# Unread 512-column matmuls in TensorE's two waits between the last output projection and the expert tables

## The chip, the cores and the metric

The kernel runs on one core of one Trainium2 chip. The metric is device time in microseconds (us) of one launch. The kernel before took 2901.69 us (median of 3 runs, 2897.95 to 2902.46).

## The reference

One layer of a streaming encoder over 4096 prompt frames and 8 streams of 16 sample frames, all in float32 with 1024 channels. What it computes, cut to what matters:

```python
h = rms_norm(x, norm1_g)
z, xbc, dt, gu, gv = split(h @ w_in)
xbc, conv_new = causal_conv(xbc, conv_prev)          # silu, width 4
y, h_final = ssd_scan(xs, dt, a, B, C, h0)           # 8 heads x 64, state 128
ssd_out  = group_rmsnorm(y * silu(z)) * ssm_norm_g
gmlp_out = gelu(gu) * (tril(W_s) @ layer_norm(gelu(gv)) + b)
x = x + concat(ssd_out, gmlp_out) @ w_out            # output projection
h2 = rms_norm(x, norm2_g)
# hierarchical MoE: top-1 of 4 groups, then top-2 of 8 SwiGLU experts in it
expert, weight = route(h2)
x = x + sum_k weight_k * (silu(h2 @ w_gate[e_k]) * (h2 @ w_up[e_k])) @ w_down[e_k]
y = rms_norm(x, final_norm_g)
```

Besides y it returns the convolution tails, the final states of the scan (`ssm_prompt`, `ssm_sample`) and the sample streams' v rows.

## The kernel before, in words

The program is written out by hand for each engine, with semaphores between the engines; nothing reorders it. It has two stages.

Stage 1 goes over 33 tiles of 128 tokens (32 of the prompt, one of the 8 sample streams). In each turn TensorE projects the next tile (`project`, `project_channels`), runs the scan and the spatial gate of this one, and ends with the output projection (`pe_out`, three blocks of columns, of which the last, YB, also holds the router's logits). VectorE adds the residual (`dve_x2`, L888), ScalarE sums the squares (`act_x2sq`, L731), GpSimd takes the root (L1134), and VectorE then picks the experts of the tile (`dve_route`, L1003 to L1026). TensorE counts the picks by two small matmuls, the rank (`pe_rank`, L532 and L533), and VectorE turns the counts into places in the experts' token lists (`dve_slots`, L1034 to L1048), which GpSimd scatters to memory.

The end of stage 1, where the change lies, is `pe_end` on TensorE. After the last output projection it runs two of the eight matmuls of the sample streams' new states (`pe_sample_update`, L553), the rank of the last tile, and the third of those matmuls. Meanwhile VectorE goes through `dve_route` and `dve_slots` for the last tile and then `dve_tables`: from the final counts it works out which 128-token block belongs to which expert. GpSimd gathers the token lists (L1480) once `row_i` is there. TensorE turns the table columns `tcol` into rows (`pe_table_rows`, L1590), waits for the lists, transposes these too (L1597), and runs the other five state matmuls, each of which waits for VectorE to have read an older one (`smp_new`, L1080). VectorE copies the tables (L1434), does three steps of the state update (L1079 and L1080), writes the lists (L1438 to L1440), and the rest. When tables and lists are there, GpSimd gathers the first blocks' rows (L1488).

Stage 2 goes over pairs of blocks of 128 slots, for at least 33 pairs, and further pairs by a branch: TensorE transposes the gathered rows (`pe_rows`, L1566), multiplies by gate and up (`pe_gate_up`, L1581, 8 matmuls of 512 columns) and by down (L1621). The expert weights arrive in four slots of SBUF by SyncE's queue; the first three experts' are loaded while stage 1 ends.

The PSUM bank that the change writes, `TB_mem[:, 0]`, is read for the last time in stage 1 by ScalarE before the last output projection, and is written next by L1566. `ident` and `cst` are constants in SBUF, loaded at the start. Each matmul of float32 in the program stands as two records, each with its own weight load, in the trace; a transpose stands as one.

Of the kernel before, what the change touches and what calls it, by code (L numbers as in the profile page):

```python
# [109 lines left out]
def after(eng, sem, n):  # L110

    if n > 0:
        eng.wait_ge(sem, n)
# [8 lines left out]
def build(nc, x_rows, x_cols, consts_in, cols_in, bcast_in, w_in, w_out, w_out_T_in, ws_in, ws_smp_in, cache_in, st_old_in,  # L122
          st_T_in, slot_in, w_exp, final_g, y_out, conv_prompt, ssm_prompt, conv_sample, ssm_sample, gmlp_v_sample):
    ctx = ExitStack()
    with ctx:
        def sb(name, shape, dt=F32):
            return ctx.enter_context(nc.sbuf_tensor(name, shape, dt))

        def ps(name, shape):
            return ctx.enter_context(nc.psum_tensor(name, shape, F32))  # L130
# [4 lines left out]
        def flat(ap):  # L135
            return ap.rearrange("p a b -> p (a b)")
# [25 lines left out]
        cst = sb("cst", [P, NCONST])  # L162
        ident, tri, stri, tri_s = (cst[:, c:c + P] for c in (C_IDENT, C_TRI, C_STRI, C_TRI_S))
# [79 lines left out]
        TB_mem = ps("TB", [P, 2, 4, P])  # L243
# [87 lines left out]
        def half(b):  # L331
            return slice(4 * b, 4 * b + 4)
# [133 lines left out]
        def pe_turn(pe, tn):  # L466
            i, u = tn.i, tn.u
            v = 1 - u
            if tn.end:
                pe_end(pe)  # L470
                return
# [54 lines left out]
        def pe_rank(pe, i, after_decay, cb_read):  # L526

            pe.wait_ge(s["pick_ready"], i)
            pe.wait_ge(s["cb_read"], cb_read)
            if after_decay:  # L530
                pe.wait_ge(s["smp_dec_out"], 1)
            nc.tensor.matmul(rk_p, stri, oh[:, 2, :], start=True, stop=True)  # L532
            nc.tensor.matmul(cnt_p, ones[:, 0:1].broadcast_to([P, P]), oh[:, 2, :], start=True, stop=True).then_inc(s["rank_done"], 1)  # L533
# [15 lines left out]
        def pe_sample_update(pe, n0, n1):  # L549

            for n in range(n0, n1):
                after(pe, s["smp_new"], n - 2)
                nc.tensor.matmul(smp_bank[n % 3], xw[:, (n // 2) * P:(n // 2 + 1) * P],  # L553
                                 flat(bmask[:, n // 4, half(n % 2), :]), start=True, stop=True).then_inc(s["states_done"], 1)

        def pe_end(pe):
            pe.wait_ge(s["smp_masks"], 3)
            pe.wait_ge(s["gated_ready"], NT)
            pe_sample_update(pe, 0, 2)
            pe_rank(pe, NT, False, NT)  # L560
            pe.wait_ge(s["lg_read"], NT)
            pe_sample_update(pe, 2, 3)

        def pe_phase1(pe):
            pe.wait_ge(ident_loaded, 16)
            pe_spread(pe, 0, TB[0], [])
            project_channels(pe, 0, 0, "xa", "proj_xa", [("x_scaled", 1)], by_block="xa_scaled")
            pe_spread(pe, 1, TB[0], [])
            project_channels(pe, 0, 1, "xb", "proj_xb", [("w_scaled", 1)])
            project(pe, 0, PB[0][:, 0:NVA], "va", "proj_va", [("w_scaled", 2), ("xa_out", 1)])  # L570
            project(pe, 0, PB[1][:, 0:NVB], "vb", "proj_vb", [("w_scaled", 3), ("xb_evicted", 1)])
            pe_router_weights(pe, 0)
            project(pe, 0, PB[0][:, :], "u", "proj_u", [("w_scaled", 4), ("va_out", 1)])
            pe_router_weights(pe, 1)
            project(pe, 0, PB[1][:, :], "z", "proj_z", [("w_scaled", 5), ("gv_out", 1)])
            pe.wait_ge(const_loaded, 16)
            pe_front_sums(pe, 0)
            pe_router_weights(pe, 2)
            pe_front_channels(pe, 0)
            over_tiles(lambda tn: pe_turn(pe, tn))  # L580
# [1271 lines left out]
```

## Time and profile before

| | |
|---|---|
| median of 3 runs | 2901.69 us |
| the profiled execution | 2901.85 us |
| its span | 2900.0 us |
| around the span | 1.85 us |
| mean granted clock | 0.992 of full |
| PE busy | 2855.1 us (98%) |
| VectorE busy | 1580.9 us (55%) |
| GpSimd busy | 870.4 us (30%) |
| ScalarE busy | 807.8 us (28%) |

The share of an engine says how much of the span it was at work. The chain of waits follows the work that ended last back to the start; what stands in it lay on the path that sets the time. In the rows of single instructions the first number is the start in us from the span's start, the second the time that the group took. PEclk is the granted clock of TensorE as a share of 2.4 GHz: 0.50 is 1.2 GHz.

### The profile page before, as it was taken

To read this page: it belongs to the slowest core of one execution; us is meant where nothing else is said; L and a number is where in the kernel's file an instruction comes from. 1 tells how busy PE (TensorE), PEld (TensorE's weight loads), DVE (VectorE), ACT (ScalarE), POOL (GpSimd) and SP (SyncE) were. 2 spreads that over 40 slices of the span, in tenths; PEclk is the share of its full clock that TensorE was granted. 3 is DMA by queue.
4 is the path that set the end of the run, shared out by engine and by line. 5 is a ranking of instruction groups with operands and counts; after the bars stand their busy time and mean duration, and the time that the engine had idled before them with its cause. 6 is when DMAs were issued, how large, how long until landed. Compare 5 with 4: busy or idle time off the path is not lost.

```text
span 2900.0 us, 38336 instructions
## 1 busy us (share of the span) xinstructions
PE 2855.1 (98%) x12809; PEld 1888.1 (65%) x12809; DVE 1580.9 (55%) x4163; ACT 807.8 (28%) x1518; POOL 870.4 (30%) x1366
## 2 busy tenths in 40 slices
PE   8999999999999999999999999989999999999997
PEld 6776777677767767777777677754444444444443
DVE  5656565556555565556565656564444444444444
ACT  2223232322332232323232322312222222222222
POOL 0121111112111211121112112114656665656665
PEclk9999999999999999999999999989999999999999
DMA  7312121221112111211121211257675667567653
GB/s 308 140 52 73 59 73 52 73 73 60 54 71 80 52 59 66 80 52 62 70 74 52 73 60 65 75 221 267 236 262 191 224 200 255 200 219 269 245 171 124
DMA packets 109623, 369.01 MB, mean 127 GB/s; under 512 B 39497, under 2 KB 41426, under 8 KB 99442
## 3 DMA queue, kind: packets, MB, share of 16 engines
q1 hardware_dynamic: 48946, 252.91, 23.9%
q0 software_dynamic: 60480, 113.57, 11.9%
q8 instruction: 112, 1.84, 0.3%
q14 instruction: 85, 0.70, 0.1%
HBM read 325.09 MB, written 140.33 MB: 160 GB/s over the span
## 4 chain that ended last, share of the span: by engine, by line
PE 97%; DMA 1%; DVE 1%; issue 0%; SPq 0%; POOL 0%; ACT 0%; POOLq 0%; DVEq 0%; ACTq 0%
PE PB L368 24%; PE PB L1581 19%; PE PB L379 16%; PE PB L463 12%; PE SS L1621 9%; PE YB L463 4%; PE TB L1566 2%; PE YB L417 2%; PE TB L357 1%; DMA arena<-in_w_in 1%; PE SS L426 1%; PE TB L440 1%; PE SS L430 1%; PE TB L404 1%; PE YB L1614 1%; PE MB L408 1%
## 5 line engine op out<-in xcount | busy, mean ns | idle before, releaser
L368 PE MATMUL PB<-arena,hT 128*128 128x512 f32 (+2 forms) x2112 | 726.7, 498 | 1.5 <-ACT xT L592 0.8
L368 PEld LDWEIGHTS PB<-arena,hT 128*128 128x128 f32 x2112 | 398.3, 191 | 269.8 <-issue 224.3
L1581 PE MATMUL PB<-arena,hT 128*128 x1296 | 569.3, 592 | 0.0
L379 PE MATMUL PB<-hT,arena 128*128 128x128 f32 x4224 | 487.1, 276 | 4.2 <-DVE arena L1096 4.2
L379 PEld LDWEIGHTS PB<-hT,arena 128*128 128x128 f32 x4224 | 481.6, 193 | 8.1 <-issue 4.5
L1581 PEld LDWEIGHTS PB<-arena,hT 128*128 128x128 f32 x1296 | 246.4, 190 | 309.2 <-issue 309.2
L1133 POOL TENSOR_SCALAR rs<-sq 128x2 f32<-128x2 f32 (+1 forms) x66 | 14.1, 213 | 1306.6 <-ACT h L731 957.1
L463 PE MATMUL PB<-arena,tT 128*128 128x274 f32 (+1 forms) x1056 | 357.8, 493 | 0.7 <-ACT tT L636 0.7
L1621 PE MATMUL SS<-arena,xdt 128*128 x640 | 287.9, 593 | 0.0
L463 PEld LDWEIGHTS PB<-arena,tT 128*128 128x128 f32 x1056 | 195.7, 190 | 140.6 <-issue 120.4
L795 DVE SCALAR_TENSOR_TENSOR xc<-xT,cols,xc 128x128 f32<-128x128 f32 x792 | 216.8, 346 | 3.5
L1621 PEld LDWEIGHTS SS<-arena,xdt 128*128 128x128 f32 x640 | 115.5, 191 | 114.7 <-issue 114.7
L1651 ACT ACTIVATE xdt<-YB 128x256 f32<-128x256 f32 x80 | 30.8, 385 | 512.1 <-PE YB L1614 512.1
L1680 DVE TENSOR_TENSOR gv<-ycat,PB 128x256 f32<-128x256 f32 x81 | 34.1, 421 | 214.0 <-ACT ycat L1646 210.3
L731 ACT ACTIVATE h<-x_res 128x1024 f32<-128x1024 f32 x33 | 34.9, 1057 | 384.6 <-DVE x_res L888 384.6
L592 ACT ACTIVATE xT<-PB 128x512 f32<-128x512 f32 x64 | 38.2, 599 | 350.0 <-PE PB L379 350.0
L463 PE MATMUL YB<-arena,tT 128*128 128x274 f32 x528 | 127.6, 394 | 0.0
L793 DVE TENSOR_SCALAR xc<-xT,cols 128x128 f32<-128x128 f32 x264 | 70.8, 342 | 94.2 <-ACT xT L592 88.2
L463 PEld LDWEIGHTS YB<-arena,tT 128*128 128x128 f32 x528 | 100.0, 190 | 22.0
L1688 DVE SCALAR_TENSOR_TENSOR arena<-arena,rs 128x1024 f32<-128x1024 f32 x80 | 102.2, 1278 | 13.5 <-POOL rs L1519 13.3
L1493 POOL DMA_INDIRECT out_y<-arena,bc x80 | 89.4, 1117 | 24.7 <-issue 23.8
L967 DVE TENSOR_TENSOR hT<-hT,TB 128x1024 f32<-128x1024 f32 x33 | 40.3, 1221 | 95.1 <-PE TB L388 95.1
(273 smaller groups left out, 3587.7 us busy)
## 6 DMA issues: line engine op xcount, KB each, us to landing
arena<-in_w_expert SPq DMA_DIRECT2D x32, 2048.0 KB, 8.9
arena<-in_w_expert SPq DMA_DIRECT2D x32, 1024.0 KB, 7.0
h_rows<-h SPq DMA_DIRECT2D x34, 512.0 KB, 2.7
x_in<-in_x_rows SPq DMA_DIRECT2D x33, 512.0 KB, 4.6
hT<-in_x_cols SPq DMA_DIRECT2D x33, 512.0 KB, 3.7
x_res<-in_x_rows SPq DMA_DIRECT2D x33, 512.0 KB, 5.2
dec<-running_sums SPq DMA_DIRECT2D x33, 512.0 KB, 3.7
first_rows<-bc SPq DMA_DIRECT2D x33, 512.0 KB, 3.9
```

Source lines behind the costliest of these rows:

```text
L368: mm = nc.tensor.matmul(out, hT[u][:, k, :], w_group(name)[:, k, :], start=k == 0, stop=k == KD - 1)
L379: mm = nc.tensor.matmul(PB[b][:, c * P:(c + 1) * P], w_block(name, c)[:, k, :], hT[u][:, k, :], start=k == 0, stop=k == KD - 1)
L417: mm = nc.tensor.matmul(bank[:, c], dec[:, h, :], xdt[:, c], start=True, stop=True)
L463: mm = nc.tensor.matmul(out_p[b], tT[:, k, :], w_out_sb[b][:, k, :], start=k == 0, stop=k == KD - 1)
L793: ins = V.tensor_scalar(dst, src, tap[:, w, c:c + 1], cols[:, R_CBIAS + c:R_CBIAS + c + 1], ALU.mult, ALU.add)
L795: ins = V.scalar_tensor_tensor(out=dst, in0=src, scalar=tap[:, w, c:c + 1], in1=dst, op0=ALU.mult, op1=ALU.add)
L967: V.tensor_tensor(hT[u][:, :, :], hT[u][:, :, :], TB[0][:, 0:1, :].broadcast_to([P, KD, P]), ALU.mult).then_inc(s["x_scaled"], 1)
L1493: nc.gpsimd.indirect_dma_start(out=dram, in_=src, in_offset=None, bounds_check=last, oob_is_err=False, out_offset=bass.IndirectOffsetOnAxi ...
L1566: mm = nc.tensor.transpose(TB[k][:, c, :], g_buf[b % GB][:, (4 * k + c) * P:(4 * k + c + 1) * P], ident)
L1581: mm = nc.tensor.matmul(PB[u][:, :], hT[u][:, k, :], arena[:, bass.ds(slot + k * 2 * DE, 2 * DE)], start=k == 0, stop=k == KD - 1)
L1621: mm = nc.tensor.matmul(SS[:, n, :], hTb[:, k, :], arena[:, bass.ds(slot + KD * 2 * DE + k * D + n * 512, 512)], start=k == 0, stop=k == 1)
L1688: V.scalar_tensor_tensor(out=f_buf[u], in0=f_buf[u], scalar=rs[:, u:u + 1], in1=gf_b, op0=ALU.mult, op1=ALU.mult).then_inc(s["fin_out"], 1)
```

## The change

`pe_end` gets two runs of plain matmuls that nothing reads: 9 between the second state matmul and the rank, and 12 after the third state matmul, at the end of stage 1. Each has the identity as its weights and 512 columns of the constants as its moving data, and writes 128x512 to a free PSUM bank. They wait for nothing and raise no semaphore. Nothing is taken away. The inserted lines move the later ones down by 7, so that L1590, L1597, L1566 and L1581 of before are L1597, L1604, L1573 and L1588 in the changed kernel.

```diff
@@ -553,13 +553,20 @@
+        def pe_idle_passes(n):
+
+            for _ in range(n):
+                nc.tensor.matmul(TB_mem[:, 0, :, :].rearrange("p a b -> p (a b)"), ident, cst[:, 0:512], start=True, stop=True)
+
         def pe_end(pe):
             pe.wait_ge(s["smp_masks"], 3)
             pe.wait_ge(s["gated_ready"], NT)
             pe_sample_update(pe, 0, 2)
+            pe_idle_passes(9)
             pe_rank(pe, NT, False, NT)
             pe.wait_ge(s["lg_read"], NT)
             pe_sample_update(pe, 2, 3)
+            pe_idle_passes(12)
```

The order of instructions on TensorE from the last block of the output projection (YB) to the five late state matmuls, as a difference (a row is a line, an operation, what it writes and reads, and how many of it stand in a row in the program):

```order
 L463 MATMUL YB<-arena,tT 128x274 x8
 L553 MATMUL SS<-arena,xw 128x512 x2
+L559 MATMUL TB<-cst 128x512 x9
 L532 MATMUL MB<-oh,cst 128x32
 L533 MATMUL MB<-oh,cst 128x32
 L553 MATMUL YB<-arena,xw 128x512
-L1590 MATMUL MB<-cst,tcol 1x128 x4
-L1597 MATMUL PB<-cst,gu 128x128 x2
+L559 MATMUL TB<-cst 128x512 x12
+L1597 MATMUL MB<-cst,tcol 1x128 x4
+L1604 MATMUL PB<-cst,gu 128x128 x2
 L553 MATMUL SS<-arena,xw 128x512 x2
```

Nothing is reordered: the rank and the third state matmul now stand behind the 9, and the two groups of transposes and the late state matmuls behind the 12 as well. The other engines' order is as before.

## Rows read from the trace of the kernel before

**Rows 1.** The page: busy time by engine, and the chain that ended last.
```profile
PE 2855.1 (98%) x12809; PEld 1888.1 (65%) x12809; DVE 1580.9 (55%) x4163; ACT 807.8 (28%) x1518; POOL 870.4 (30%) x1366
PE 97%; DMA 1%; DVE 1%; issue 0%; SPq 0%; POOL 0%; ACT 0%; POOLq 0%; DVEq 0%; ACTq 0%
```
**Rows 2.** Waits of PE: in total, times, longest.
```profile
PE MB L1590 <- DVE tcol L1425: 6.8, 1, 6.8
PE MB L532 <- DVE oh L1026: 5.1, 1, 5.1
```
**Rows 3.** Timeline of PE: start, us, line, operation, records, idle before.
```profile
1929.52 0.30 PE L532 MATMUL MB<-oh,cst 128*128 128x32 f32 x2
1929.88 3.95 PE L463 MATMUL YB<-arena,tT 128*128 128x274 f32 x16
1933.66 1.88 PE L553 MATMUL SS<-arena,xw 128*128 128x512 f32 x4
1940.62 0.64 PE L532 MATMUL MB<-oh,cst 128*128 128x32 f32 x2 [5.08 <-DVE oh L1026]
1941.49 2.06 PE L553 MATMUL YB<-arena,xw 128*128 128x512 f32 x2
```
**Rows 4.** Chain of waits in order of time: start, us, what.
```profile
1875.29 6.87 PE PB L368 x16
...
1930.04 3.80 PE YB L463 x16
...
1941.61 0.16 DVE slots L1041
1941.77 0.15 DVE rk L1043
...
1950.12 0.17 DVE tcol L1425
...
1950.33 1.02 PE MB L1590 x4
...
1951.38 0.06 DVE yb L1434
...
1958.87 5.38 DMA x_in<-h_rows,bc
...
1964.96 0.66 PE TB L1566 x4
1965.62 13.73 PE PB L1581 x32
```
**Rows 5.** Timeline of the transposes and of the late state matmuls.
```profile
1917.07 1.03 PE L357 MATMUL TB<-cst,ycat 128*128 128x128 f32 x8
1952.63 0.70 PE L1597 MATMUL PB<-cst,gu 128*128 128x128 f32 x2 [1.29 <-DMA gu<-slot_tokens,row_i]
1953.43 3.78 PE L553 MATMUL SS<-arena,xw 128*128 128x512 f32 x4
1959.05 1.13 PE L553 MATMUL SS<-arena,xw 128*128 128x512 f32 x2 [0.36 <-DVE arena L1080]
1960.38 1.12 PE L553 MATMUL SS<-arena,xw 128*128 128x512 f32 x2 [0.20 <-DVE arena L1080]
```
**Rows 6.** Windows: stretch, busy us of each engine (records), PEclk, DMA share, GB/s.
```profile
42.00:44.00 2.00, 2.00 (x3) 0.68 (x2) 1.43 (x5) 1.32 (x2) 1.11 (x5) 0.50 1.13 467
1900.00:1935.50 35.50, 34.76 (x139) 22.89 (x137) 14.49 (x48) 4.62 (x12) 3.66 (x6) 1.00 0.55 222
1937.00:1938.00 1.00, 0.00 (x0) 0.00 (x0) 0.86 (x6) 0.00 (x0) 0.00 (x0) 0.93 0.75 246
1943.60:1950.30 6.70, 0.00 (x0) 0.00 (x0) 5.96 (x35) 0.00 (x0) 2.47 (x3) 0.50 0.62 230
1958.00:1959.00 1.00, 0.69 (x2) 0.00 (x0) 0.97 (x3) 0.00 (x0) 0.70 (x2) 0.83 0.00 0
1965.00:2865.00 900.00, 900.00 (x2682) 442.90 (x2683) 416.99 (x476) 225.45 (x469) 532.73 (x541) 1.00 0.65 225
```

## The prediction, made before the changed kernel ran

> **What bounds the kernel now.** I read the page first: TensorE is busy 98% of the span and makes up 97% of the chain that ended last [rows 1]. So an instruction added to TensorE costs its full time, unless it lies where TensorE waits. TensorE's list of waits says where that is: among its few long ones are the two that this change fills, 5.1 us before the rank (L532, waiting for the experts picked by VectorE) and 6.8 us before the table rows (L1590, waiting for VectorE's `tcol`) [rows 2]. In that stretch the chain of waits leaves TensorE: from the end of the last output projection, 1930.04 + 3.80, to the table rows at 1950.33 it runs through VectorE, ScalarE and GpSimd; after four transposes on TensorE it runs on through VectorE's table copy and list writes to GpSimd's gather of the first rows, and it is back on TensorE for good at 1965.62 [rows 4]. From there to 2865 TensorE is busy in all of 900.00 us [rows 6]: whatever this stretch ends later, the kernel ends later, one for one.
>
> The windows tell the clock: full up to 1935.5, with a mean of 0.93 in 1937 to 1938, and 0.50 (1.2 GHz) in the second wait. It is back at 2.4 GHz in the course of 1958 to 1959 (mean 0.83) and stays there in the whole expert stage [rows 6]. So 2.4 GHz is there when the long work starts. What the low clock costs now is only what TensorE does on the path between 1938 and 1958.
>
> **The size of a pass.** The change is 9 and 12 matmuls of 512 columns, but a float32 matmul of the program stands as two records in the trace: the last 8 matmuls of the YB block are "x16", the two state matmuls "x4" [rows 3]. The price of a record of 512 columns at the full clock is 6.87 / 16 = 0.429 us, from a group of 16 in the chain; 13.73 / 32 of the expert stage gives the same [rows 4]. Hence a matmul of 512 columns is 0.859 us, 9 of them are 18 x 0.429 = 7.73 us, and 12 are 24 x 0.429 = 10.30 us. Against waits of 5.1 and 6.8 us [rows 2] both are too long. This is the step on which my forecast rests.
>
> The Trainium skill, TensorE: Matmul & The Clock Gate, section "Wait — 56ns, not 53.3ns?", gives 215.7 ns from start to start for a matmul of 512 columns at the high clock. The trace disagrees for float32: 429 ns a record, and two of them. By that figure of the Trainium skill the 9 would be an estimated 1.94 us and the 12 an estimated 2.59 us, and both would fit in their waits.
>
> **First run of passes.** The two state matmuls start at 1933.66 [rows 3], four records are 1.72 us, so the passes start streaming at 1935.38. With 18 records the rank comes at 1943.11, where it came at 1940.62 [rows 3]. Queued behind the passes are the rank, the third state matmul and everything after. For the rank VectorE waits. Before, its four records went at the low clock and VectorE read them at 1941.77, right behind the step before it, which started at 1941.61 and ran 0.16 us [rows 4]: the rank had next to no slack. Behind a full-clock stream the rank of the previous tile started at 1929.52, and the YB block streamed from 1930.04 [rows 3, 4], so it takes 0.52 us. VectorE reads the rank at 1943.11 + 0.52 + 0.04 = 1943.67, about 1.9 us later than now. What the higher clock saves of the rank is inside this. The scatter and the list gather (GpSimd) move with it. So does `tcol`, to 1950.12 + 0.17 + 1.9 = 1952.2.
>
> **Second run.** TensorE does not wait for VectorE there. From the rank's start to the next matmul's is 1929.88 - 1929.52 = 0.36 us [rows 3], so the third state matmul starts at 1943.47. Its two records take 0.86, and the 24 records of the passes 10.30: the table rows can start at 1954.63. That is 2.4 us after `tcol`, so here TensorE is what comes last, and the 1.9 us of the first run are contained in this, not added. The four transposes take 1.02 now, at 1.2 GHz [rows 4]. At 2.4 GHz eight of the same width took 1.03 with their tail [rows 5], so four lie between half of that, 0.52, and 0.66, what the last four L1566 took [rows 4]. I take 0.55. VectorE copies the tables at 1954.63 + 0.55 + 0.03 = 1955.21 instead of 1951.38 [rows 4]: 3.8 us late.
>
> **What follows.** The lists' transposes wait for the list gather, which landed before 1952.63 [rows 5]; 1.9 us later is 1954.5, still before TensorE is free at 1955.2, so the gather is no new wait. VectorE's three steps of state update and the list writes start from the table copy, and come 3.8 us later, and so do the gather of rows and stage 2. The late state matmuls are paced by VectorE's reads (the last one waited 0.20 for one), and the last ends at 1961.50, while the chain is still in the gather [rows 4, 5]; so their higher clock saves nothing. Nobody reads the bank that the passes write, and no queue but TensorE's own has anything new in it.
>
> **Sum.** TensorE's own chain from 1935.38: 7.73 + 0.36 + 0.86 + 10.30 + 0.58 = 19.83, to 1955.21, against 1951.38 before: +3.8 us. The span becomes 2903.8, and the profiled execution 2901.85 + 3.8 = 2905.7. The median of the runs shown is 0.16 us below that execution, so I predict 2901.69 + 3.8 = 2905.5 us, 0.13% more. The bounds: the price of a record is the same in two stages, so the 42 records are certain to about 0.1. The hand-over from the rank is 0.36 at 2.4 GHz and was 1941.49 - 1940.62 = 0.87 at 1.2 GHz [rows 3], the transposes lie between 0.52 and 1.02. Together +3.7 to +4.9.
>
> A measurement of this kernel can tell about 0.2% from no change, 5.8 us. So by size this is "the same", with the slower side near.
>
> **Rivals.**
>
> *The passes fit.* If a pass with identity weights cost one record and not two, or half a record's time, the first run would be 3.9 us and end at 1939.2, the second 5.2 us and end near 1947.0, both before they are waited for. Then the change does what its place suggests: the clock stays up and the table's transposes take 0.55 instead of 1.02. The rank saves nothing, since VectorE comes to it at 1941.77 anyway. Result -0.4 us: 2901.3. For it speaks only that transposes by the same identity are one record each [rows 5]. Against it: the state matmuls and the rank, plain matmuls like these, are two. Chance 0.08. The figure of the Trainium skill (TensorE: Matmul & The Clock Gate, same section) would lead to this case too.
>
> *Part of it is absorbed.* The delay could shrink on the way, if the row gather, 5.38 us in the chain [rows 4], is faster when it starts later. Up to 2 us could go: 2903.5 to 2905. Against it: the 5.38 is a gather that starts after a stretch with no DMA traffic (0.00 in 1958 to 1959 [rows 6]), and nothing that it could collide with is moved away. Chance 0.10.
>
> *The slower side: the clock at the head of the expert stage.* Now it rises at about 1958.3, 4.9 us after the late state matmuls begin at 1953.43 [rows 5, 6]. With the passes TensorE is busy up to 1955.8 and then sparse for some 10 us (five matmuls of 0.86, with gaps between them). It could be granted 1.2 GHz in that stretch and enter the gate and up matmuls with it. If the clock then stays low for as long as there, 4.9 us, they cost 2.45 us more: +6.3, 2908.0, slower by 0.22%. For it: the clock fell some 2.3 us after TensorE ran dry, between 1937 and 1938. Against it: in the trace of before the sparse end of the same stretch (state matmuls at 1959.05 and 1960.38, transposes up to 1965.62 [rows 4, 5]) lies behind the rise, and the clock is 1.00 from 1965 [rows 6]. It decides from a fall between 1955.8 and 1969. Chance 0.11.
>
> *The slower side, extreme: the passes themselves run at 1.2 GHz.* The clock has stood at 0.50 under a TensorE that was busy in every record's time, at 42 to 44 us [rows 6]. If it fell at 1937.9 as now, 5.9 records would be done and 12.1 left at 0.858: rank at 1948.3, table rows at 1948.3 + 0.87 + 1.72 + 20.6 = 1971.5, and VectorE at 1972.5: +21 us, 2922.8. Against it: at 1900 to 1935.5, with such streams of 512 and 274 columns, the clock was 1.00. Chance 0.04.
>
> **How the numbers follow.** The forecast as worked out has 0.67, the others 0.08, 0.10, 0.11 and 0.04. Slower by over 0.2% means past 2907.5: the extreme case whole, about two thirds of the clock case, and the share of the forecast's case in which the medians scatter by 2 us (the three runs lie 4.5 us apart), about 0.11 in all of it: 0.04 + 0.07 + 0.10 = 0.21. Faster by over 0.2% would need 2895.9, out of reach of every case except by scatter: 0.02. Same: 0.77. The range, 2901.2 to 2908.6, holds the fitting case and the clock case at its edges and leaves out the extreme one.
>
> **What would show it.** The profile after should have 18 and 24 records of L559 at 0.429 from start to start, 42 in all, the rank at 1943.1 with no wait before it, the table rows at 1954.6 with no wait before them, and PEclk 1.00 from 1935 to 1955. Both waits of TensorE, 5.1 and 6.8, should be gone, VectorE should wait for TensorE about 1.9 us at `rk` (L1050 there) and some 3 us at the table copy, and the first gate and up matmul should come at about 1969.3. I am wrong in the size of a pass if the records are 21 or half as long, wrong in the path if the table copy is 3.8 us late and the gate and up matmuls are not, and wrong about the clock if PEclk is under 1.00 between 1960 and 1975.

## The result, and the profile after

The changed kernel took 2906.95 us (median of 17 runs, 2901.72 to 2908.76), the kernel before 2900.51 us (17 runs, 2897.95 to 2902.66). The ratio is 1.0017, with a 95% interval from 1.0011 to 1.0023: slower by 4.9 us (3.2 to 6.7). The forecast was +3.8 us and 2905.5 us. The size of the delay in the profile is as forecast; the median of the runs lies higher than that, 6.4 us above the median of before, and a good part of the experiments went into why.

The profiled execution took 2905.47 us, with a span of 2903.6 us.

The timeline of TensorE (start, us, line, operation, records, idle before), beside [rows 3, 5]:

```profile
1932.92 1.88 PE L553 MATMUL SS<-arena,xw 128*128 128x512 f32 x4
1934.63 7.89 PE L559 MATMUL TB<-cst 128*128 128x512 f32 x18
1942.36 0.30 PE L532 MATMUL MB<-oh,cst 128*128 128x32 f32 x2
...
1942.72 1.10 PE L553 MATMUL YB<-arena,xw 128*128 128x512 f32 x2
1943.66 10.46 PE L559 MATMUL TB<-cst 128*128 128x512 f32 x24
1953.96 0.60 PE L1597 MATMUL MB<-cst,tcol 128*1 128x128 f32 x4
...
1956.65 3.40 PE L553 MATMUL SS<-arena,xw 128*128 128x512 f32 x4 [1.85 <-DVE arena L1087]
```

9 and 12 passes are 18 and 24 records. Neither the rank nor the table rows has an idle time before it. In this execution stage 1 ended 0.74 us earlier (first state matmul at 1932.92, before at 1933.66), so starts are compared as distances from that matmul.

The chain of waits in order of time (start, us, what), beside [rows 4]:

```profile
1934.79 7.72 PE TB L559 x18
...
1943.82 10.30 PE TB L559 x24
1954.12 0.45 PE MB L1597 x4
...
1954.60 0.07 DVE yb L1441
...
1962.09 5.74 DMA x_in<-h_rows,bc
...
1967.87 1.09 PE TB L1573 x8
```

The chain no longer leaves TensorE between the output projection and the table copy. 18 records are 7.72 us and 24 are 10.30, 0.429 each. The table copy stands 1954.60 - 1932.92 = 21.68 us behind the first state matmul; before it was 1951.38 - 1933.66 = 17.72. That is +3.96.

VectorE's timeline shows the other side of the same wait:

```profile
1951.32 0.15 DVE L1432 TENSOR_SCALAR tcol<-rt 128x1 f32<-128x1 f32 x1
...
1954.60 0.68 DVE L1441 CAST yb<-MB 1x512 int32<-1x512 f32 x1 [2.38 <-PE MB L1597]
```

TensorE's list of waits (in total, times, longest), beside [rows 2]:

```profile
PE SS L553 <- DVE arena L1087: 3.0, 3, 1.9
PE TB L1573 <- DMA x_in<-h_rows,bc: 2.1, 2, 1.6
```

The 6.8 and the 5.1 us are gone, and what comes up is a gap of 1.85 us in front of the late state matmuls. Before, these began at 1953.43, right behind the list transposes at 1952.63 + 0.70 [rows 5]. The windows (stretch, busy us of each engine with its records, PEclk, DMA share, GB/s), beside [rows 6]:

```profile
1935.00:1955.00 20.00, 19.80 (x54) 9.08 (x52) 13.18 (x74) 0.21 (x1) 3.66 (x5) 1.00 0.64 232
1957.00:1958.00 1.00, 1.00 (x3) 0.02 (x1) 0.96 (x3) 0.00 (x0) 0.00 (x0) 0.67 0.00 0
1958.00:1960.00 2.00, 2.00 (x4) 0.92 (x4) 1.93 (x6) 0.00 (x0) 0.00 (x0) 0.50 0.00 0
1960.00:1961.00 1.00, 1.00 (x3) 0.18 (x1) 0.90 (x5) 0.00 (x0) 0.29 (x1) 0.62 0.00 0
1965.00:1980.00 15.00, 13.19 (x43) 6.77 (x44) 4.15 (x7) 2.86 (x4) 2.66 (x3) 1.00 0.84 314
```

The passes do hold the clock at 2.4 GHz. Then it falls at about 1957.3 and is back in the course of 1960 to 1961: behind the passes, in the sparse stretch, and before the expert stage.

### The profile page after: what moved, and what is told of

The parts are those of the page before. It is cut to its first block, busy times and chain, and to the rows that moved or that the text cites. A ratio compares the mean times of both kernels' runs of the same rounds, so it can differ in the third digit from the quotient of the medians.

```text
span 2903.6 us, 38420 instructions
## 1 busy us (share of the span) xinstructions
PE 2868.3 (99%) x12851; PEld 1892.7 (65%) x12851; DVE 1581.1 (54%) x4163; ACT 807.7 (28%) x1518; POOL 870.0 (30%) x1366
## 4 chain that ended last, share of the span: by engine, by line
PE 98%; DMA 1%; issue 0%; DVE 0%; SPq 0%; POOL 0%; POOLq 0%; ACT 0%; DVEq 0%; ACTq 0%
PE PB L368 24%; PE PB L1588 19%; PE PB L379 16%; PE PB L463 12%; PE SS L1628 9%; PE YB L463 4%; PE TB L1573 2%; PE YB L417 2%; PE TB L357 1%; DMA arena<-in_w_in 1%; PE SS L426 1%; PE TB L440 1%; PE SS L430 1%; PE TB L404 1%; PE TB L559 1%; PE YB L1621 1%
## 5 line engine op out<-in xcount | busy, mean ns | idle before, releaser
L1588 PE MATMUL PB<-arena,hT 128*128 x1296 | 569.3, 592 | 0.2 <-issue 0.2
L1588 PEld LDWEIGHTS PB<-arena,hT 128*128 128x128 f32 x1296 | 246.1, 190 | 310.0 <-issue 310.0
L463 PEld LDWEIGHTS YB<-arena,tT 128*128 128x128 f32 x528 | 99.9, 189 | 22.1
```

What stands on the lines that cost most here:

```text
L463: mm = nc.tensor.matmul(out_p[b], tT[:, k, :], w_out_sb[b][:, k, :], start=k == 0, stop=k == KD - 1)
L1588: mm = nc.tensor.matmul(PB[u][:, :], hT[u][:, k, :], arena[:, bass.ds(slot + k * 2 * DE, 2 * DE)], start=k == 0, stop=k == KD - 1)
```

## Experiments

Each kernel's profile gives four starts: the first state matmul, VectorE's reading of the rank (`rk`), the table copy, and the transposes of the first hidden block, which follow the first two gate and up products (YB by `gv`). As distances from the first state matmul, in us:

| kernel | first state matmul at | rank read | table copy | hidden block | median and range of runs (n) |
|---|---|---|---|---|---|
| before | 1933.66 | 8.06 | 17.72 | 45.53 | 2900.51, 2897.95 to 2902.66 (17) |
| changed | 1932.92 | 10.00 | 21.68 | 49.61 | 2906.95, 2901.72 to 2908.76 (17) |
| e1, 9 and 0 | 1930.84 | 10.00 | 19.65 | 47.63 | 2903.19, 2900.87 to 2904.14 (11) |
| e2, 0 and 12 | 1932.54 | 8.04 | 21.39 | 49.18 | 2905.00, 2903.01 to 2906.32 (11) |
| e3, 6 and 9 | 1932.37 | 8.01 | 17.24 | 45.03 | 2900.87, 2898.86 to 2903.07 (11) |
| e4, 9 and 9 | 1932.66 | 10.00 | 19.23 | 47.02 | 2902.35, 2899.69 to 2904.02 (11) |
| f1, changed again | 1932.33 | 10.01 | 21.68 | 49.49 | 2906.80, 2901.35 to 2908.78 (11) |
| f2, late gaps filled | 1932.41 | 10.00 | 21.68 | 49.49 | 2904.29, 2902.15 to 2906.89 (11) |
| f3, 18 and 24 | 1932.69 | 17.73 | 39.71 | 67.50 | 2922.99, 2922.72 to 2924.16 (5) |
| f4, 6 and 9, gaps | 1933.50 | 8.02 | 17.27 | 45.07 | 2901.01, 2898.97 to 2902.11 (11) |
| g1, changed, one run | 1933.20 | 10.01 | 21.68 | 49.48 | 2905.77 (1) |
| g2, changed, one run | 1931.63 | 10.01 | 21.69 | 49.48 | 2904.58 (1) |
| g3, first gap only | 1934.34 | 10.01 | 21.68 | 51.00 | 2907.37, 2901.86 to 2908.26 (11) |
| g4, later gaps only | 1933.96 | 10.01 | 21.69 | 49.48 | 2904.32, 2901.51 to 2906.78 (11) |

### Each run of passes by itself

```diff
-            pe_idle_passes(12)
+            pe_idle_passes(0)
```

> Only the 9 passes before the rank, none after the third state matmul. Theory (each pass is two records of 0.429 us, and TensorE's own row of work decides): the rank comes 1.9 us late, VectorE is delayed from there, and the table rows wait for it again, at the low clock: table copy +1.9 us, time +1.9 us. Rival (delays of the two runs add, and the second is worth the rest of what the median moved): the same +1.9 here, but then the kernel with the second run alone must make up +4.5 or more. Rival (the passes fit in the wait): no change.

Measured: rank +1.94, table copy +1.93; time 1.0008 (0.9999 to 1.0017), or +2.2 us between the medians. TensorE waits for the table columns again, and the transposes are at 1.2 GHz as before:

```profile
1949.44 1.01 PE L1597 MATMUL MB<-cst,tcol 128*1 128x128 f32 x4 [7.69 <-DVE tcol L1432]
```

```diff
-            pe_idle_passes(9)
+            pe_idle_passes(0)
```

> Only the 12 passes after the third state matmul. Theory: the rank is at its old place and at the low clock; the third state matmul ends near 1943.3, and the 24 records begin at 1.2 GHz, the clock rises some 5 us after TensorE is busy again; 3 records at 0.858 and 21 at 0.429 end near 1955, against the 1950.3 at which the table rows are wanted: table copy about +4 us, as late as with both runs, so the two runs' delays do not add. Rival (delays add): about +2 us (the 3.8 of both less the 1.9 of the first).

Measured: rank -0.02, table copy +3.67; time 1.0014 (1.0005 to 1.0023), +4.05 between the medians. The passes begin at 1.2 GHz, and have 2.4 GHz for most of their length:

```profile
1940.36 2.05 PE L553 MATMUL YB<-arena,xw 128*128 128x512 f32 x2
1942.21 11.25 PE L559 MATMUL TB<-cst 128*128 128x512 f32 x24
1953.29 0.60 PE L1597 MATMUL MB<-cst,tcol 128*1 128x128 f32 x4
```

```profile
1942.00:1943.00 1.00, 1.00 (x2) 0.34 (x1) 0.87 (x5) 0.00 (x0) 0.99 (x1) 0.50 0.99 418
1943.00:1944.00 1.00, 1.00 (x3) 0.49 (x2) 0.87 (x6) 0.00 (x0) 0.71 (x1) 0.61 0.86 361
1944.00:1946.00 2.00, 2.00 (x7) 0.81 (x6) 1.86 (x7) 0.00 (x0) 0.25 (x1) 1.00 0.16 58
```

So 1.93 by the first run alone and 3.67 by the second alone make 3.96 together, not 5.60: they do not add, because TensorE is last in one place only. The rival that they add is out.

### Passes that fit

```diff
-            pe_idle_passes(9)
+            pe_idle_passes(6)
-            pe_idle_passes(12)
+            pe_idle_passes(9)
```

> 6 passes in the first wait and 9 in the second: 12 x 0.429 = 5.15 us from 1935.38, to 1940.5, just before the rank is wanted, and 18 x 0.429 = 7.7 us from 1941.8, to 1949.6, before the table rows are wanted at 1950.3. Theory: nothing is delayed, the clock stays up and the four table transposes take 0.45 us less: table copy -0.4 us, time -0.4 us, no more than that. Rival (the clock kept up is worth more, since the expert stage starts with it): -2 us or more. Rival (the passes disturb VectorE or the DMAs whatever their length): slower by 1 us or more although no wait is overrun.

Measured: table copy -0.48; time 0.9999 (0.9990 to 1.0008). The rank is on time, and TensorE is idle for a moment before the table rows, which are done at the high clock:

```profile
1934.08 5.31 PE L559 MATMUL TB<-cst 128*128 128x512 f32 x12
1939.31 0.41 PE L532 MATMUL MB<-oh,cst 128*128 128x32 f32 x2
...
1940.72 7.89 PE L559 MATMUL TB<-cst 128*128 128x512 f32 x18
1948.98 0.60 PE L1597 MATMUL MB<-cst,tcol 128*1 128x128 f32 x4 [0.37 <-DVE tcol L1432]
```

The half microsecond is in the trace and too small for the runs. VectorE's copy of the table has no idle time before it any more and starts 0.84 us behind the last `tcol` (before: 1.26, of which 0.35 waiting for TensorE), so VectorE's own steps now set when it comes:

```profile
1948.77 0.15 DVE L1432 TENSOR_SCALAR tcol<-rt 128x1 f32<-128x1 f32 x1
1949.61 0.68 DVE L1441 CAST yb<-MB 1x512 int32<-1x512 f32 x1
```

The passes inside a wait disturb nothing. The clock kept up through the two waits is worth no more than this half microsecond; it fell once more behind them (PEclk 0.50 in 1953 to 1955), so the rival of a clock held up to the expert stage is left to f4 below.

### 9 and 9

```diff
-            pe_idle_passes(12)
+            pe_idle_passes(9)
```

> 9 and 9 passes. Theory: the rank is 1.9 us late as with 9 and 12; the second run ends near 1944.3 + 7.7 = 1952.05, and VectorE's table columns come at 1952.2, so that VectorE is last again: table copy +1.5 us (1.9 less 0.4 for the higher clock), time +1.5. Rival (every pass costs its 0.86 us wherever it stands): 3 passes less than 9 and 12 give -2.6 us, table copy +1.3, hardly different here; what tells them apart is who waits: with the theory TensorE waits some 0.2 us before the table rows.

Measured: rank +1.94, table copy +1.51; time 1.0004 (0.9995 to 1.0013), +1.4 between the medians. Three passes less give 2.45 us, a little less than their 2.58, since VectorE is last again. The profile has no idle time of TensorE in front of the table rows: the passes end at 1943.40 + 7.72 = 1951.12 and `tcol` at 1951.05 + 0.15. Of TensorE's wait, 0.2 us expected, there is nothing to see. Who is last shows on VectorE's side:

```profile
1951.05 0.15 DVE L1432 TENSOR_SCALAR tcol<-rt 128x1 f32<-128x1 f32 x1
1951.89 0.68 DVE L1441 CAST yb<-MB 1x512 int32<-1x512 f32 x1
```

The copy is again 0.84 us behind `tcol` with no idle time before it, where the changed kernel has 2.38 us of waiting for TensorE. So VectorE decides here, and the delay is the rank's 1.94 less the 0.42 between 1.26 and 0.84: 1.52, with 1.51 measured.

### Doubled

```diff
-            pe_idle_passes(9)
+            pe_idle_passes(18)
-            pe_idle_passes(12)
+            pe_idle_passes(24)
```

> 18 and 24 passes in place of 9 and 12. Theory (two records of 0.429 us a pass, all on the path from the first to the last): 42 more records, 18.0 us, on top of the changed kernel: table copy at +21.9 us, time 2905 + 18 = about 2923. Rival (a pass costs one record, 0.43, and the rest of the delay comes from elsewhere): +9 us.

Measured: rank read +9.67, table copy +21.99; time 1.0079 (1.0066 to 1.0093), 2922.99 us.

```profile
1934.40 15.61 PE L559 MATMUL TB<-cst 128*128 128x512 f32 x36
...
1951.16 20.76 PE L559 MATMUL TB<-cst 128*128 128x512 f32 x48
1971.76 0.60 PE L1597 MATMUL MB<-cst,tcol 128*1 128x128 f32 x4
```

The table copy is 18.03 us later than in the changed kernel, 42 records of 0.429. The runs lie 22.1 us above the median of before. Taking 18.0 off that leaves 4.1 us for the 9 and 12 passes, which is the 3.96 of the trace, and not the 6 between the medians of the changed kernel and before.

### Where the rest of the median comes from

The runs of the changed kernel fall into two groups: 8 from 2901.72 to 2905.47, 9 from 2906.95 to 2908.76.

> The changed kernel again, as it is. Its profile had the table copy 3.9 us late and a span 3.6 us longer, but its runs lay between 2901.7 and 2908.8, with a median 6.4 us above that of before. Theory A (the executions differ in where the clock is low after the passes, at the head of the expert stage; the granted mean of the long ones is 0.995 and of the short ones 0.997): the spread is there again, 5 us or more, and long runs have the lower mean clock. Rival B (that set of runs was drawn high by chance): median within +3.3 to +4.6 of before, spread no wider than that of before.

Measured: 2906.80 us, ratio 1.0018 (1.0009 to 1.0027); 5 of 11 runs up to 2905.2 and 6 from 2906.8. Chance (B) is out. The granted mean was 0.996 to 0.997 in the short ones and 0.995 to 0.996 in the long ones. The profile again was of a short one, with the clock at 1.00 from 1955 to 1980:

```profile
1955.00:1980.00 25.00, 19.75 (x54) 8.58 (x55) 13.23 (x26) 2.86 (x4) 6.03 (x6) 1.00 0.57 202
```

The next kernel fills TensorE's gaps behind the passes with further ones, into PB[0], which is free there:

```diff
             mm.then_inc(s["lists_T"], 1)
-            pe_sample_update(pe, 3, 8)
+            pe_late_passes(2)
+            pe_sample_update(pe, 3, 6)
+            pe_late_passes(1)
+            pe_sample_update(pe, 6, 8)
...
             pe_rows(pe, 0)
+            pe_late_passes(1)
             pe_rows(pe, 1)
```

> 9 and 12 passes as in the changed kernel, and 2 passes behind the list transposes, 1 ahead of the seventh state matmul and 1 between the transposes of the first two gathered blocks, each in a gap of TensorE. Theory A (a low clock after the passes makes the long executions): the clock is up throughout, the late state matmuls run at 0.43 a record, and the runs are 2 us or so shorter in the median than the changed kernel's, with less spread. Rival B: the same time as the changed kernel within 0.5 us, since the chain runs through VectorE and the gather there.

Measured: 2904.29 us, ratio 1.0012 (1.0003 to 1.0021), 2.5 us below the changed kernel in the same set of runs; one run of 11 over 2906.5. Table copy and hidden block are at the same distances as in f1. So the chain is not shortened, and yet the long executions are rare.

> The changed kernel again, one profile, to catch a long execution (2906.8 us or more: 16 of the 28 so far). Theory A: in a long one the granted clock is 1.2 GHz in a part of the gate and up matmuls, between 1964 and 1980, and the time from the table copy to the second block is 2 to 3 us longer than in a short one (2905 or less), where it is 2.4 GHz there. Rival B: the difference lies in stage 1 or late in the expert stage, and the stretch from the table copy on is the same.

> The same once more, for the same reason; with the same expectations of both theories.

Measured: 2905.77 and 2904.58 us, neither a long one (the first lies just above the short group's 2905.47). (The number of long executions up to then was 15 of 28, not 16.) In g1 the clock was low from 1957 to 1961 and high in the expert stage, in g2 it was high throughout. They did not catch what they were meant to.

Then the gaps apart. First only the one behind the list transposes:

```diff
             mm.then_inc(s["lists_T"], 1)
+            pe_late_passes(2)
             pe_sample_update(pe, 3, 8)
```

> 9 and 12 passes, and 2 passes in the gap behind the list transposes only (1.85 us in the changed kernel's profile). Theory A1 (that gap is what lets the clock fall): the long executions go away as with all gaps filled, median about 2904.3. Theory A2 (the later gaps, before the seventh state matmul and between the transposes of the first two gathered blocks, do it): executions of 2907 and more remain, median near 2906.

Measured: 2907.37 us, ratio 1.0017 (1.0008 to 1.0026), and 7 runs of 11 over 2906.5. Its profile is of a long execution, 2908.26 us. The timeline of TensorE, and the windows:

```profile
1968.95 1.76 PE L1578 MATMUL TB<-cst,x_in 128*128 128x128 f32 x8 [1.24 <-DMA x_in<-h_rows,bc]
1970.50 15.00 PE L1593 MATMUL PB<-arena,hT 128*128 x32
```

```profile
1968.00:1969.00 1.00, 0.05 (x1) 0.05 (x1) 0.96 (x3) 0.00 (x0) 0.70 (x2) 1.00 0.86 311
1969.00:1970.00 1.00, 1.00 (x6) 0.79 (x7) 0.54 (x1) 0.19 (x1) 0.68 (x1) 0.65 0.98 332
1970.00:1971.00 1.00, 1.00 (x5) 0.84 (x4) 0.25 (x1) 0.98 (x2) 0.00 (x0) 0.50 1.19 459
1971.00:1972.00 1.00, 1.00 (x2) 0.34 (x1) 0.44 (x1) 0.71 (x1) 0.00 (x0) 0.50 1.03 426
1972.00:1973.00 1.00, 1.00 (x3) 0.44 (x2) 0.00 (x0) 0.00 (x0) 0.00 (x0) 0.65 1.06 455
```

Here the clock falls at about 1969.3, at the transposes of the second gathered block, and is back at about 1972.7, low for 3.4 us. The transposes take 1.76 where the changed kernel's profile has 1.09, and the first 32 gate and up records 15.00 where [rows 4] have 13.73 (the chain's own figure here is 14.79). The hidden block comes 51.00 us behind the first state matmul instead of 49.48 to 49.61: the fall costs 1.4 to 1.5 us. That is not all that makes this execution long. Its span is 3.8 us longer than that of f1 (2906.4 against 2902.6), and 2.0 of them had passed before the first state matmul (1934.34 against 1932.33).

Then only the later gaps:

```diff
-            pe_sample_update(pe, 3, 8)
+            pe_sample_update(pe, 3, 6)
+            pe_late_passes(1)
+            pe_sample_update(pe, 6, 8)
...
             pe_rows(pe, 0)
+            pe_late_passes(1)
             pe_rows(pe, 1)
```

> 9 and 12 passes, and 1 pass before the seventh state matmul and 1 between the transposes of the first two gathered blocks. Theory A2: the long executions go away, median about 2904.3. Theory A1: they remain, median near 2906, since the gap behind the list transposes is still open.

Measured: 2904.32 us, ratio 1.0010 (1.0001 to 1.0019), one run of 11 over 2906.5. The gap behind the list transposes is open, and the clock fell there in the profile:

```profile
1957.70 3.40 PE L553 MATMUL SS<-arena,xw 128*128 128x512 f32 x4 [1.85 <-DVE arena L1092]
```

That costs nothing, since the late state matmuls are not on the path: hidden block at 49.48. This profile is of the one run over 2906.5, 2906.78 us, and its gate and up matmuls had the full clock: its span is 2.3 us longer than that of f1, 1.6 of them before the first state matmul (1933.96 against 1932.33) and 0.7 behind the hidden block. So an execution can be over 2906.5 without the fall of g3.

Taken together: with the later gaps open (changed kernel, f1, the two single profiles, g3) 22 of 41 executions were over 2906.5 us, with them filled (f2, g4) 2 of 22. The limit was chosen after the runs, and the two later gaps were not filled apart.

The last kernel has the fitting 6 and 9 passes and one pass in each of three later gaps:

```diff
-            pe_idle_passes(9)
+            pe_idle_passes(6)
-            pe_idle_passes(12)
+            pe_idle_passes(9)
...
             mm.then_inc(s["tab_rows"], 1)
+            pe_late_passes(1)
...
-            pe_sample_update(pe, 3, 8)
+            pe_sample_update(pe, 3, 6)
+            pe_late_passes(1)
+            pe_sample_update(pe, 6, 8)
...
             pe_rows(pe, 0)
+            pe_late_passes(1)
             pe_rows(pe, 1)
```

> 6 and 9 passes, which fit in the waits, and 1 pass ahead of the list transposes, 1 ahead of the seventh state matmul and 1 between the transposes of the first two gathered blocks. Theory: nothing on the path is touched except the four table transposes at the high clock: -0.4 us, no more, the clock 1.00 from 1935 to the end. Rival (a clock held up to the gate and up matmuls is worth something in the expert stage): -2 us.

Measured: table copy -0.45, time 1.0001 (0.9992 to 1.0010). The clock is 1.00 in every window from 1936 on up to the kernel's last 20 us, and it is worth nothing that can be measured. No version beats the kernel before.

## Why the prediction was right, and what it left out

**The size of a pass** was right: 18 and 24 records of 0.429 us. **The first run** was right to 0.01 us: the rank was read 1.94 us late (forecast 1.95 from 1943.67 - 1941.72, the start of that read). **The second run** too: the table copy was forecast 3.83 late and came 3.96 late. Half of the 0.13 is in the four transposes, which began at 1953.96 and were read at 1954.60, 0.64 against the 0.58 allowed; the other half came before them. That TensorE's own row of work and not VectorE decides there is shown by e1 and e2, 1.93 and 3.67 alone and 3.96 together, and by e4, where three passes less hand the last place back to VectorE.

**One for one to the end** held as well. The hidden block is +3.95 to +4.08 in the four profiles of the changed kernel, doubling the passes moved table copy and hidden block by a further 18 us, and the run time to 22.1 us above before.

**The high clock saves nothing more** was right, with e3 and f4 as evidence: -0.45 to -0.48 us in the trace and no difference in time.

**The time itself was nearer than the delay, by luck.** 2905.5 is 1.45 us under the measured median, while +3.8 is 2.6 under the difference of the medians: the three runs of before that I started from had a median of 2901.69, and all 17 have 2900.51. My bounds for the delay, +3.7 to +4.9, hold the trace's 3.96 and, at their edge, the 4.9 of the ratio; the +6.4 between the medians is outside. (In the working of the chances the share for scatter is 0.11 in one place and 0.10 in the sum.)

**What I mis-sized** is not a term of the sum but the case that the sum left out, the clock at the head of the expert stage. I gave it 0.11 and 2.45 us, as if a kernel had it or had it not. In fact the clock behind the passes differs between executions of the same kernel, and in the changed kernel about half of them are long. By my own sign I was wrong about the clock: PEclk is 0.62 in 1960 to 1961 already in the profile of the changed kernel, though at no cost there. The measured price of a fall on the gate and up matmuls, in the one profile that caught it, was 1.4 to 1.5 us for a low clock of 3.4 us; I had taken a low of 4.9 us from the trace of before. It is a part of why the median (+6.4) stands above the trace (+4.0), and not all: the mean of the 17 runs is +5.4 us, 1.4 above the trace, and if each of the 9 long runs had such a fall, it would lift the mean by an estimated 9/17 of 1.5, 0.8 us. Where I argued against it, that the clock was 1.00 from 1965 in the trace of before, I read one execution as if it were a property of the kernel. The place that I named, between 1955.8 and 1969, is about where the clock did fall (at 1957.3 in the changed kernel's profile, at 1969.3 in g3's), and the counts of long runs point at the later part of it, the gaps before the seventh state matmul and between the transposes of two gathered blocks.

**What stays open.** One profile shows the fall, and the rest is inferred from how often runs are long. The long group lies some 2 to 4 us above the short one, and 1.5 us of that is shown to come from a fall. Stage 1 gives more: up to 3.5 us between profiles (last section), 2.0 of the 3.8 us by which g3's span is longer than f1's, and 1.6 of the 2.3 us of g4's. How the nine long runs of the changed kernel divide between the two is not known. And e2, e4 and f3 have the later gaps open too, and no long runs: e2 and e4 none over 2906.4 in 11 each, e2 with a table copy only 0.3 us earlier than the changed kernel's, and the five runs of f3 lie within 1.5 us, none over 2906.5 + 18.0. So open gaps do not suffice, and what makes a fall land on the gate and up matmuls in one kernel and not in the next was not settled. By the Trainium skill, TensorE: Matmul & The Clock Gate, section "What's actually happening", the window by which the clock is set runs free of the kernel; that would make the same gaps count or not from one execution to the next. The profiles agree so far as the clock in the sparse stretch differs between four executions of the same kernel (low in two, 1.00 in two), but no run here controls it.

## What to carry to other kernels

Count filler in records, not in lines of the program: read from the trace how many records a matmul of that type makes and what one costs there, and compare that with the wait. Filler that fits its wait is free, filler that overruns it delays by the overrun at the one place where TensorE comes last, and two overruns in a row do not add. A clock kept up is worth only what TensorE does on the path in the stretch that was low, here 0.5 us, after which VectorE's own steps came last; and one profile shows one execution's clock, so that the spread of the runs has to be read beside it.

## What was not expected of the hardware

The clock of stage 1's first 80 us differs from execution to execution of the same instructions, and the end of stage 1 moves with it. In the windows from 30 to 90 us, of e1 and then of g3:

```profile
30.00:90.00 60.00, 59.06 (x348) 47.77 (x347) 33.35 (x93) 15.94 (x26) 8.36 (x30) 0.97 0.70 278
```

```profile
30.00:90.00 60.00, 59.21 (x323) 45.91 (x323) 30.34 (x88) 16.75 (x27) 8.38 (x30) 0.91 0.69 271
```

In the first, TensorE gets 348 records done in 60 us, in the second 323. The first state matmul, 1850 us later, is at 1930.84 in e1 and at 1934.34 in g3. 0.06 of 60 us is 3.6 us of clock, and the starts differ by 3.5; from 90 to 1930 us the mean is 1.00 in all fourteen profiles. They fall into three groups: with a mean of 0.91 in 30 to 90 us the first state matmul is at 1933.50 to 1934.34 (four profiles, before among them), with 0.94 at 1932.33 to 1933.20 (eight, the changed kernel among them), with 0.97 at 1930.84 and 1931.63 (e1 and g2). These 3.5 us are in a stretch that no edit here touches, beside the 4.7 us by which the runs of the kernel before differ.

A matmul by the identity cost the same 0.429 us a record as one by real weights, and the clock was at 2.4 GHz in all of the 20 us that passes filled.
